# Expert results scaled on their way out of PSUM, earlier clearing of slot rows, and a moved activation in a two-layer diffusion backbone

## What is computed

```python
def moe(h, router_w, router_b, w_gate, w_up, w_down):
    ...
    w = w / jnp.sum(w, axis=-1, keepdims=True)
    gates = jnp.sum(jax.nn.one_hot(idx, N_EXPERTS, dtype=F32) * w[..., None], axis=1)
    hg = jnp.einsum('td,edf->tef', t, w_gate)
    hu = jnp.einsum('td,edf->tef', t, w_up)
    act = jax.nn.silu(hg) * hu * gates[..., None].astype(t.dtype)
    out = jnp.einsum('tef,efd->td', act, w_down)
...
        xp = xp + g1p * yp
        xs = xs + g1s * ys
        xp = xp + g2p * moe(adaln(xp, norm2_g[layer], sh2p, sc2p), ...)
        xs = xs + g2s * moe(adaln(xs, norm2_g[layer], sh2s, sc2s), ...)
```

## Time and profile before

| | us |
|---|---|
| median of 3 runs | 1613.66 |
| lowest, highest | 1610.9, 1620.55 |
| profiled execution | 1610.85 |
| its span, first to last instruction | 1608.9 |
| busy: PE, DVE, ACT, POOL | 1462.1, 589.2, 561.4, 180.5 |

### The profile page before, as it was taken

One profiled execution on the slowest core, in us unless ns is written; L12 is line 12 of the kernel. 1 busy time (PEld: TensorE's weight loads), 2 busy tenths in 40 slices (PEclk: granted clock), 3 DMA queues, 4 the chain that ended last, 5 costly groups with the idle time before them and its releaser, 6 DMA issues.

```text
span 1608.9 us, 19000 instructions
## 1 busy us (share of the span) xinstructions
PE 1462.1 (91%) x7515; PEld 744.2 (46%) x7515; DVE 589.2 (37%) x926; ACT 561.4 (35%) x1233; POOL 180.5 (11%) x179
## 2 busy tenths in 40 slices
PE   6999799999979999798999899899889999899980
PEld 3444454444454333475455455455454445533330
DVE  1234555653450000273545545545543133400004
ACT  4112444441112222344573573573580001122212
POOL 0112000000010000300400400410311100200002
PEclk9999999999999999899999999999999999999995
DMA  9503666469279999613232232133055020999985
GB/s 347 219 1 112 231 198 227 158 201 382 88 296 360 411 417 411 241 57 122 67 116 105 66 119 105 66 118 105 13 183 210 14 104 25 371 403 418 408 337 209
DMA packets 121331, 323.28 MB, mean 201 GB/s; under 512 B 7814, under 2 KB 37206, under 8 KB 110998
## 3 DMA queue, kind: packets, MB, share of 16 engines
q1 hardware_dynamic: 100396, 260.33, 43.9%
q0 software_dynamic: 8496, 31.17, 5.2%
q10 hardware_dynamic: 12352, 30.58, 4.8%
HBM read 279.05 MB, written 42.99 MB: 200 GB/s over the span
## 4 chain that ended last, share of the span: by engine, by line
PE 79%; DVE 10%; ACT 4%; DMA 3%; issue 3%; SPq 0%; POOL 0%; ACTq 0%; DVEq 0%; POOLq 0%
PE ps L959 12%; PE ps L1060 10%; PE ps L1220 9%; PE ps L1115 8%; PE ps L739 7%; PE ps L980 6%; PE ps L908 4%; PE ps L1062 3%; PE ps L686 2%; PE ps L829 2%; PE ps L813 2%; PE ps L1199 2%; PE ps L943 2%; PE ps L933 1%; PE ps L1191 1%
## 5 line engine op out<-in xcount | busy, mean ns | idle before, releaser
L959 PE MATMUL ps<-mem 128*32 128x512 f32 (+1 forms) x1408 | 198.1, 594 | 1.9 <-ACT mem L1399 1.9
L1060 PE MATMUL ps<-mem 128*128 128x512 f32 x384 | 170.0, 596 | 1.0 <-ACT mem L1589 1.0
L1220 PE MATMUL ps<-mem 128*128 128x512 f32 x320 | 139.0, 593 | 3.2 <-issue 2.7
L1115 PE MATMUL ps<-mem 128*128 128x512 f32 x320 | 140.7, 593 | 0.1
L1917 DVE TENSOR_TENSOR mem<-ps,mem 128x256 f32<-128x256 f32 x28 | 11.9, 424 | 336.5 <-ACT mem L1408 336.5
L1987 DVE SCALAR_TENSOR_TENSOR mem<-mem 128x642 f32<-128x642 f32 x96 | 92.7, 965 | 86.6 <-ACT mem L1513 84.0
L959 PEld LDWEIGHTS ps<-mem 128*32 128x32 f32 (+1 forms) x1408 | 59.0, 117 | 123.1 <-issue 122.9
L1060 PEld LDWEIGHTS ps<-mem 128*128 128x128 f32 x384 | 71.6, 191 | 82.3 <-issue 80.9
L739 PE MATMUL ps<-mem 128*128 128x512 f32 x240 | 106.4, 600 | 1.9 <-DVE mem L1691 1.9
L980 PE MATMUL ps<-mem 128*32 128x512 f32 (+1 forms) x704 | 103.6, 601 | 4.2 <-ACT mem L1412 4.2
L1549 ACT ACTIVATE mem<-mem,small 128x128 f32<-128x128 f32 x320 | 95.1, 391 | 26.1 <-DMA mem<-cum_rows 26.1
(11 more groups left out here) (318 smaller groups left out, 2034.5 us busy)
## 6 DMA issues: line engine op xcount, KB each, us to landing
mem<-in_mod_w SPq DMA_DIRECT2D x24, 2048.0 KB, 9.0
mem<-in_expert_w_gate SPq DMA_DIRECT2D x40, 1024.0 KB, 10.6
mem<-in_expert_w_up SPq DMA_DIRECT2D x40, 1024.0 KB, 13.7
mem<-in_expert_w_down SPq DMA_DIRECT2D x40, 1024.0 KB, 15.5
mem<-cum_rows SPq DMA_DIRECT2D x40, 512.0 KB, 5.5
slot_rows<-mem ACTq DMA_DIRECT2D x28, 512.0 KB, 8.0
mem<-slot_rows ACTq DMA_DIRECT2D x26, 512.0 KB, 11.2
slot_rows<-mem SPq DMA_DIRECT2D x1, 12288.0 KB, 52.9
```

Of the source, the lines that this page charges most:

```text
L959: last = nc.tensor.matmul(ps[c:c + w, 2 + j, :], XGT[j][:, k, c:c + w], GUW[l][m][:, :, k, :], start=(k == 0), stop=(k == KD - 1))
L1060: nc.tensor.matmul(ps[:, b, :], w[:, k, :], HT[:, k, SEQ:TOK], start=(k == 0), stop=(k == KD - 1))
L1115: last = nc.tensor.matmul(ps[:, ZBANK[t], :], HT[:, k, t * P:(t + 1) * P], WZ[2 * k // KD][:, k % (KD // 2), :], start=(k == 0), stop=(k = ...
L1220: last = nc.tensor.matmul(ps[:, 4 + n % 4, :], YT[b][:, k, t * P:(t + 1) * P], w[:, k, :], start=(b == 0 and k == 0), stop=(b == 1 and k = ...
```

## The change

1. **Gates at eviction.** `H` rows are 1040 floats apart (`HX`), and three extra columns carry a token's two gates (as second gate, and first minus second) and its first slot number, negated for tile 0. They are scattered with the row. `rows_out` copies the three columns of a pack's rows into `gates`; pack 0 gets them by a small DMA of its own. `factor_row` on DVE makes from them, per pack, a 128x1024 factor `GROW`: gate times the modulation row of the right kind of token. The result leaves PSUM on DVE as a product with `GROW` and is stored to a separate tensor `slot_results`. The gathers read that, ACT's scaling is gone, and DVE's combine is two additions.
2. **Router.** Before the scatter and `PICK`, DVE computes these columns (two 160-element products, one reduction, three small writes, and one more small operation earlier); one small subtraction goes there, and six operations after the routing go.
3. **Slot rows cleared early.** The 12 MB DMA is replaced by 24 pieces of 0.53 MB, and 12 of 0.52 MB for the upper half of `slot_results`, each issued behind one of the 18 modulation weight loads of attention.
4. **Fillers.** 11 for 10 before the routing; 14 of 256 columns for four of 512 after it; two per surplus pack; 7 of 192 columns ahead of the wait for the first gather, 14 after it, and 4 or 1 of them between tiles for 3 of 256.
5. **Norm between the layers.** DVE turns two column blocks and ACT six, from different PSUM banks. ACT takes a square root of no use right after the packs, so that the table is loaded; POOL's wait before the last gathers becomes one for that, before tile 3, and its marker operation between tiles 3 and 4 goes.
6. **conv_out(0, 0)** runs ahead of ACT's copies of the cumulative sums.

```diff
-        H = page(34, NT * D).rearrange("p (t n) -> p t n", t=NT)
+        WIDE = D + 16
+        HX = page(34, NT * WIDE).rearrange("p (t n) -> p t n", t=NT)
+        H = HX[:, :, 0:D]
...
+        gates = page(40.75, 12).rearrange("p (a b) -> p a b", a=4)
+        signed = page(40.8, 8)
+        rowno = sb("rowno", [P, 1])
+        XG = [page(43 + i * 33 / 32, WIDE) for i in range(2)]
+        XGT = [page(45 + 1 / 16 + i, D).rearrange("p (k n) -> p k n", k=KD) for i in range(2)]
+        YO = [page(47 + 1 / 16 + i, D) for i in range(2)]
+        SG_, AC, AT = ([page(39 + 3 / 32 + 0.75 * i + 0.25 * j, FF) for i in range(2)] for j in range(3))
+        GROW = [page(41 + i, D) for i in range(2)]
...
-        xs_d = nc.dram_tensor("slot_rows", (ROWS, D), F32, kind="Internal").ap()
+        xs_d = nc.dram_tensor("slot_rows", (ROWS + 1, WIDE), F32, kind="Internal").ap()
+        ys_d = nc.dram_tensor("slot_results", (ROWS + 1, D), F32, kind="Internal").ap()
+        results = ys_d[1:1 + ROWS].rearrange("(a p) n -> a p n", p=P)
+        slots = xs_d[1:1 + ROWS].rearrange("(a p) n -> a p n", p=P)
...
+        def turned_at(t, k):
+            return (4 + t % 2) * 512 + k * P if k < 2 else (t % 2) * 1024 + (k - 2) * P
...
             for r0, rounds, l, b0 in ((0, 3, 0, 6), (3, 6, 1, 0)):
                 with sp.Fori(0, rounds) as i:
                     for m, j in enumerate((0, 2)):
                         sp.wait_ge(s_wused[j], i + (r0 + 1))
                         sp.dma_start(WS[j], wv[l][i * 2 + (b0 + m)]).then_inc(s_w[j], 16)
+                        if l == 0:
+                            for h in range(2):
+                                sp.dma_start(xs_c[i * 4 + (2 * m + h)], zeros[0:104].unsqueeze(1).to_broadcast([104, 5, 256])).then_inc(s_rows, 16)
+                        else:
+                            sp.dma_start(xs_c[i * 2 + (12 + m)], zeros[0:104].unsqueeze(1).to_broadcast([104, 5, 256])).then_inc(s_rows, 16)
+                            sp.dma_start(ys_c[i * 2 + (12 + m)], zeros.unsqueeze(1).to_broadcast([P, 4, 256])).then_inc(s_rows, 16)
                 if l == 0:
                     load_wo(1)
             sp.wait_ge(s_wused[0], 10)
             load_wo(0)


-            sp.wait_ge(s_zero, 2)
-            sp.dma_start(xs_d.rearrange("(p a) (b n) -> p (a b) n", p=P, n=256),
-                         zeros.unsqueeze(1).to_broadcast([P, ROWS // P * 4, 256])).then_inc(s_rows, 16)
+            sp.dma_start(xs_d[0:1].rearrange("o (c m) -> (o c) m", m=WIDE // 5), zeros[0:5, 0:WIDE // 5]).then_inc(s_rows, 16)
+            sp.dma_start(ys_d[0:1].rearrange("o (c m) -> (o c) m", m=256), zeros[0:4, :]).then_inc(s_rows, 16)
...
+                sp.dma_start(gates[:, 0, :], slots[0][:, D:D + 3]).then_inc(ES["g0"], 16)
...
-                fill(7, 10)
-                pe.wait_ge(ES["sel"], l + 1)
+                fill(7, 11)
+                pe.wait_ge(ES["route"], 4 * l + 1)
...
-                for k in range(4):
-                    nc.tensor.matmul(ps[:, 7, :], ident, X[:, k, 0:512], start=True, stop=True)
+                fill(7, 14)
...
                         gate_up(t[j], j, *halves[j])
+                        fill(7, 1)
                         act_turned(t[j], j)
+                        fill(7, 1)
                         down(t[j], j, *halves[j])
...
+            fill(6, 7, 320, 192)
             pe.wait_ge(ES["gat"][0], 32)
-            fill(4, 14)
+            fill(6, 14, 320, 192)
             for t in range(NT):
                 if t >= 1:
-                    fill(4, 3)
+                    fill(6, 4 if t == 1 else 1, 320, 192)
...
+                def rows_out(t, j, place):
                     act.wait_ge(pk["xt"], t + (dx + 1))
+                    nc.scalar.activation(gates[:, place, :], XG[j][:, D:D + 3], ACT.Copy)
                     nc.scalar.activation(XGT[j], psf[:, 0:1024].rearrange("p (k n) -> p k n", k=KD), ACT.Copy)\
                         .then_inc(pk["xtc"], 1)

-                def load_rows(t, j):
+                def load_rows(t, j, turned):
                     if t < PACKS + 2:
+                        act.wait_ge(pk["xtc"], turned + (dx + 1))
...
-                def result_out(t, j, stores, pack):
-                    act.wait_ge(pk["dn"], t + 1)
-                    if not early(t):
-                        act.wait_ge(pk["yst"][j], stores * 16)
-                    nc.scalar.activation(YO[j], psf[:, 5 * 512:5 * 512 + D], ACT.Copy).then_inc(pk["ycopy"], 1)
+                def result_out(t, j, pack):
                     act.wait_ge(pk["ycopy"], t + 1)
-                    act.dma_start(slots[pack], YO[j]).then_inc(pk["yst"][j], 16)
-
-                s0 = 0 if l == 0 else act.snap(trips_of(act, 0) + PACKS // 2)
+                    act.dma_start(results[pack], YO[j]).then_inc(pk["yst"][j], 16)
...
+                nc.scalar.activation(ssq[:, 6:7], eps[:, :], ACT.Sqrt).then_inc(s_partc, 1)
+                act.wait_ge(s_partc, 3 * l + 4)
...
-                    for k in range(KD // 2, KD):
-                        at = (t % 2) * 1024 + k * P
+                    for k in range(2, KD):
+                        at = turned_at(t, k)
...
-                        act.wait_ge(ES["gat"][t], 32 * (l + 1))
-                        nc.scalar.activation(GY[t][0], GY[t][0], ACT.Copy, scale=gate2[:, 0, t:t + 1]).then_inc(ES["wa"], 1)
...
+            conv_out(0, 0)
             act.wait_ge(s_pre_pe, 4)
...
-            conv_out(0, 0)
             for g in range(SG):
...
+                order(V_.tensor_scalar(wsum[:, 0:1], wsum[:, 0:1], -1.0, None, ALU.mult))
...
-                order(V_.tensor_scalar(slotm, slotf[:, :, :], 1.0, None, ALU.subtract))
-                V_.tensor_copy(sloti[:, :, :], slotm).then_inc(ES["slot"], 1)
+                V_.tensor_copy(sloti[:, :, :], slotf[:, :, :])
+                of = [v.rearrange("p (a t e) -> p a t e", a=2, t=NT) for v in (route[:, 320:320 + 2 * NT * NE], route[:, 640:640 + 2 * NT * NE])]
+                order(V_.tensor_tensor(of[0], spot.unsqueeze(1).to_broadcast([P, 2, NT, NE]),
+                                       slotf[:, :, :].unsqueeze(3).to_broadcast([P, 2, NT, NE]), ALU.is_equal))
+                order(V_.tensor_tensor(of[1], of[0], weighted.unsqueeze(1).to_broadcast([P, 2, NT, NE]), ALU.mult))
+                order(V_.tensor_reduce(pairs, of[1], AX.X, ALU.add))
+                V_.tensor_copy(HX[:, :, D], pairs[:, 1])
+                V_.tensor_copy(HX[:, :, D + 2], slotf[:, 0, :])
+                V_.tensor_tensor(HX[:, :, D + 1], pairs[:, 0], pairs[:, 1], ALU.subtract).then_inc(ES["route"], 1)
...
-                for a in range(2):
-                    order(V_.tensor_tensor(mine, spot, slotf[:, a, :].unsqueeze(2).to_broadcast([P, NT, NE]), ALU.is_equal))
-                    order(V_.tensor_tensor(mine, mine, weighted, ALU.mult))
-                    order(V_.tensor_reduce(gate2[:, a, :], mine, AX.X, ALU.add))
...
+                def factor_row(j, place, first_row):
+                    order(V_.tensor_scalar(signed[:, 0:1], gates[:, place, 2:3], first_row, rowno[:, :], ALU.subtract, ALU.is_equal))
+                    order(V_.scalar_tensor_tensor(signed[:, 0:1], gates[:, place, 1:2], signed[:, 0:1], gates[:, place, 0:1],
+                                                  op0=ALU.mult, op1=ALU.add))
+                    V_.tensor_scalar(signed[:, 1:2], signed[:, 0:1], -1.0, 0.0, ALU.mult, ALU.max)
+                    order(V_.tensor_scalar(signed[:, 0:1], signed[:, 0:1], 0.0, None, ALU.max))
+                    order(V_.tensor_scalar(GROW[j], MB[1][:, 2, 1, :], signed[:, 0:1], None, ALU.mult))
+                    order(V_.scalar_tensor_tensor(GROW[j], MB[1][:, 2, 0, :], signed[:, 1:2], GROW[j], op0=ALU.mult, op1=ALU.add))
+
+                def result(t, j, stores):
+                    if not early(t):
+                        dve.wait_ge(pk["yst"][j], stores * 16)
+                    dve.wait_ge(pk["dn"], t + 1)
+                    V_.tensor_tensor(YO[j], psf[:, 5 * 512:5 * 512 + D], GROW[j], ALU.mult).then_inc(pk["ycopy"], 1)
+
+                activations(d0, 0)
+                dve.wait_ge(ES["g0"], 16 * (l + 1))
+                factor_row(0, 0, 1.0)
+                dve.wait_ge(pk["xtc"], d0 + (dx + 2))
+                factor_row(1, 1, P + 1.0)
                 for t in range(PACKS):
-                    activations(d0 + t, t % 2)
-                dve.wait_ge(ES["np"], l + 1)
+                    if t + 1 < PACKS:
+                        activations(d0 + (t + 1), (t + 1) % 2)
+                    result(d0 + t, t % 2, s0 + t // 2)
+                    if t + 2 < PACKS:
+                        dve.wait_ge(pk["ycopy"], d0 + (t + 1))
+                        dve.wait_ge(pk["xtc"], d0 + (t + 2 + dx + 1))
+                        factor_row(t % 2, (t + 2) % 4, (t + 2) * P + 1.0)
...
+                    factors_done(3)
+                    dve.wait_ge(pk["ycopy"], dve.snap(i * 2 + d0 + PACKS))
```

(24 more changed lines are left out.)

120 lines of the change are left out of this document (68 added, 52 removed).

## The result

| | kernel before | changed kernel |
|---|---|---|
| median of 20 executions, us | 1617.45 | 1608.77 |
| lowest and highest | 1608.70, 1620.65 | 1598.79, 1620.30 |
| ratio, 95% interval | | 0.9953 (0.9938 to 0.9969) |
| profiled execution, us | 1610.85 | 1610.52 |

By the ratio the change gains 7.6 us (5 to 10), by the two medians 8.7; both are under 1%. A median of 1600.2, with 13.5 gained, was forecast. The two profiled executions are equally long, because the first of them lay 6.6 us under its kernel's median. So the comparison goes stage by stage.

What follows compares the result with a forecast made beforehand. PE, holding 79% of the chain, was taken as the bound, with gains only where it waits. Terms 2.7 - 0.3 - 6.6 - 5.3 - 4.3 + 0.3 = -13.5 gave 1597.4 on the profiled 1610.85, 1600.2 on the median; range 1592 to 1608.

Steps and rivals of the forecast that it cites:

- between the layers: Combine and norm between layers: DVE's tile falls to about 3.95 us, line 1060 comes at 699.7; -6.6 us, bounds -5 and -9.
- conv_out: the wait: First convolution: PE waits about 0.6 us instead of 4.59 for the silu behind ACT's logarithm; -4.0 us.
- conv_out: the clock: First convolution: the clock drop after PE's wait, costing 1.5 us, should go with it; 1.3 us taken.
- clearing early: Attention's weight loads, 160 to 348 us: 19 MB of clearing joins them; +0.3 us, bounds 0 and 3.
- the 1.35: Router, each layer: new DVE operations ahead of the scatter and PICK cost +1.35 us, bounds 1.0 and 2.0.
- I book nothing for the fillers: Router: faster 80 products gain nothing, since PE would only wait at line 943 for slot rows; 0 us.
- rival A: Pack 1's slot rows arrive late: scatter 2 us longer per layer, then half clock; 7 us more, 1607; chance 0.13.
- the 1.7 that I took off for the low stretch at 643.0: Layer 0's surplus packs: two fillers per pack should spare the clock drop at 643.0, worth 1.7 us.
- Rival C: Packs become bound by DMA through dearer 4160-byte rows, kernel slower than before; at twice the row cost 1631; chance 0.04.
- Now arrival binds: Between layers: tile 4's second gather lands at 687.3, additions end at 689.8, line 1060 follows 9.9 us later.
- Rival D: Between layers: in_proj weights queue with the gathers, which land at 691 not 687, leaving -3; 1604; chance 0.13.
- With two passes DVE keeps up with arrival: Kernel's end: last addition 2.5 us behind the last landing, plus 0.6 from the marker; -4.3 us, bounds -3.2 and -5.5.

Runs made afterwards that it cites:

- stores_late: Changed kernel with SP's five output stores waiting for the gathers of all five tiles in layer 1; ratio 0.9958 to the kernel before.
- conv_back: Changed kernel with conv_out(0, 0) put back behind the sums' copies, logarithm and stores on ACT; median 1615.1 us, ratio 0.9984 to the kernel before.

## Why the prediction missed

The forecast of 1600.2 was 8.6 us too low. **3.8 of it is the base.** I put the profiled execution 2.8 under its kernel's median of three; over 20 executions it is 6.6. Its clock was 0.973, the mean of this kernel is 0.968. The sum of -13.5 on 1617.45 would have been 1604. **The other 5 to 6 are the sum.** Stage by stage, each value a mean over the profiled executions in which no edit touches that stage (four of the kernel before and its copies, up to eight of changed and its copies):

| term | forecast | measured |
|---|---|---|
| routers and packs with what surrounds them, to the first gather, two layers | +2.4 | +7.7 |
| between the layers, to line 1102's end | -6.6 | -4.2 |
| conv_out: the wait | -4.0 | -4.0 |
| conv_out: the clock | -1.3 | -1.5 |
| end | -4.3 | -2.4 |
| clearing early | +0.3 | 0, compared at equal time at low clock |

**Router: the price was right, and the wait beside it was not booked.** From the end of line 1867 (1853 before) to line 949 (933) it is 9.80 to 9.96 us, 8.53 before: +1.27 to +1.43 for the 1.35. Line 959 comes 34.8 us after the router's fillers begin, 34.9 forecast. The failing sentence is "I book nothing for the fillers": the slot rows' way is fixed (17.5 us of scatter, then the load), so faster products buy only a stand, and the stand costs the clock in the packs. That was this step's upper end, 2 us more per layer, and rival A's consequence by another cause. The packs of layer 0 took 165.5 to 165.7 in six of six executions with a stand of 2.5 to 3.0, and 163.0 in all four in which it was filled. Layer 1's took 162.9 in all four of before, and 164.7 to 165.7 in seven of eight changed ones. The rows in the first profile of changed hide it: there layer 1 took 163.3, behind a stand of 0.36. And the 1.7 that I took off for the low stretch at 643.0 was worth half: it stood there in two of four executions of the kernel before.

Rival A itself was wrong on the scatter of layer 0: it took 17.49 us from its first issue to the load that waits for it, 17.56 before. In layer 1 it was right in part: 16.6 to 18.4 us in 13 executions with the wide rows, 17.8 in the mean, against 16.6 to 17.2 and 17.0 in four before. These 0.8 us lengthen the stand; whether the wide rows make them was not tested. The Trainium skill (DMA: Bandwidth & Descriptors, How a descriptor splits into AXI transactions) lets a row that starts off a 256-byte boundary fetch an extra partial transaction; whatever 4160-byte rows cost by it, the scatter of layer 0 does not show.

**Packs and surplus packs.** DVE's busy time in layer 1's packs went from 5.9 to 59 us, and ACT's from 36 to 25, without a trace on PE: 163.2 for 162.9 where the clock is full, for the +0.5 forecast. From the last down product to the first gather it is 5.5 for 4.76 in layer 0 and 5.03 for 4.73 in layer 1 (forecast 0.2). Rival C fell: the packs keep 403 GB/s at share 1.01 and do not become longer by it.

**Between the layers.** The step "Now arrival binds: tile 4's second gather ... lands 9.75 later" was right: counted from the first gather, 22.6 us was forecast, and tile 4 landed at 22.5 to 23.5 in seven executions (686.54 + 11.9 less 675.12 is 23.3 in the first). Its additions ended 25.0 to 26.0 behind the first gather, for the 25.1 forecast. What took the gain back is PE at half clock for 5.4 to 6.8 us on the products behind the last addition. Four of seven executions show it (12.2 to 13.6 us from the last addition to line 1079), three do not (9.1 to 10.2, for the 9.9 forecast). In those three the first gather to line 1079 is 34.1 to 36.2, and the forecast was 35.0. So the mechanism and the size were right without the low stretch: there the whole stage gains 6.8 in the mean. The lower bound was mis-sized, "-5 if a clock drop falls into the shorter gaps": the drop fell in the majority, and with it only 2.2 are left. What brings it there, no run shows. Rival D had the right cause in part: the weights do queue with the gathers, and late weights give 2 us, but tile 4 landed at most 1 us later than forecast, not 4.

**conv_out.** Right on the wait, 0.63 for "about 0.6", and on the clock behind it. From line 1157's start to the end of the next 16 products it is 7.63 us in every execution with the move; in three of the kernel before it is 9.0 to 9.3 (line 1138), and in the first of them these products take 7.95, where the changed kernel's take 7.03:

```profile
740.12 7.95 PE L1060 MATMUL ps<-mem 128*128 128x512 f32 x16
```

By three pairs of medians the move is worth 4.8, 6.1 and 8.7 us, around the booked 5.3, each with an interval of about 4. It carries the change: the other stages of the table come to +1.1 together, and conv_back, the change without it, is not clear of the kernel before.

**End.** The step "With two passes DVE keeps up with arrival: 1595.0 + 2.5" failed: it kept up, but arrival moved. Against the first gather, the last landing is at 19.1 to 20.2 in four executions before and 21.1 to 21.8 in eleven now, since the output stores leave as soon as tiles are ready and share the DMA engines with the gathers that are left. That is shown by stores_late, where it is 17.6. The 0.6 for the marker was wrong too: without it one gather of tile 4 still takes 1.84 to issue (1.89 in rows 8), so the marker was not its cause, and in the first profile the last gather is issued only 0.3 us earlier. What the cause is, stays open. The prediction also misread the queue: behind the landing at 1595.03 DVE had 6.2 us of work, at 3.7 per tile the rest of tile 3 and tile 4, and not "three passes of four tiles"; the sum does not use that.

**What stays open.** The measured stages add up to -4.4, where the ratio says -7.6 and the medians -8.7. The rest must lie in stages that the change doesn't touch or in how often the clock falls in executions without a profile: over all executions the mean granted clock is 0.968 before and 0.971 in changed, and within one kernel 0.001 of it goes with about 1.2 us. Which stage it belongs to, four and eight profiles cannot say.

## What to carry to other kernels

Before an engine is made faster, ask for the next arrival: if a fixed transfer ends at the same time, the engine only stands, and the stand is paid a second time in the clock of the work behind it. Put fillers directly ahead of the wait, where the stand is, and not ahead of the work that leads to it. Where a combine becomes arrival-bound, look at which transfers its own first result releases; and take the base of a sum from many executions, since one profile of this kernel lay 6.6 us off. Give each part of a change a run of its own: here moving one activation gained as much as all of it.

## What the runs showed of the hardware

- The clock's low stretches are bound to a place with a chance, not to a kernel: at the same code, the start and the attention took 451 to 459 us, and two executions of the changed kernel agreed to 0.2 us until 743 and ended 12.9 apart.
- A stand of PE of 2.5 to 3.0 us was followed by granted clock 0.5 on the next products in six of six executions (layer 0); with 2.4 us of fillers in it and 0.35 to 0.5 left, in none of three. In layer 1 a stand of 1.4 to 1.9 us was followed by 3.4 us at half clock in four of four, one of 3.2 to 3.6 us by 6.1 to 6.4 us in three of three, and one of up to 1.2 us by none in ten of ten.
- The DMA engines carried gathers, stores and weights together at 400 to 437 GB/s in the busiest slices; the last gather of the kernel landed 5.4 us after its issue with the output stores held back and 9.25 with those of three tiles under way.
